# Rounding the last block's later weights in three products, with remainders on GpSimd, a tenth extra expert tile and filling matmuls in the router

## The reference, cut to what matters

```python
aff = softmax(h @ w_router)                      # 256 x 16
g, idx = top_k(aff.swapaxes(1, 2), 32)           # each expert takes 32 tokens
xs = h[idx]
y = (silu(xs @ w_gate[e]) * (xs @ w_up[e])) @ w_down[e] * g
x = x + g_f * scatter_add(y, idx)
```

```python
h = rmsnorm(x); x = x + concat(y_m, y_a) @ w_out           # y_m: mLSTM "hm", y_a: causal attention "oa"
h = rmsnorm(x)
q = rmsnorm(h @ wq_x);  k, v = (rmsnorm(mem) @ wkv_x)      # memory of 256 rows, k normed
x = x + softmax(q k^T) v @ wo_x
h = rmsnorm(x); x = x + square(relu(h @ w_ff1)) @ w_ff2    # width 4096
```

## Time and profile before

| | us |
|---|---|
| median of 3 runs | 1678.0 (1674.99 to 1681.05) |
| the profiled execution: its time | 1678.73 |
| its span, first to last instruction | 1676.9 |
| PE busy in the span | 1334.8 (80%) |
| DVE, ACT, POOL busy | 547.2, 348.4, 27.9 |
| bytes moved | 548.36 MB, mean 327 GB/s |
| mean granted clock of PE | 0.886 of full |

### The profile page before, as it was taken

How to read it: one execution, slowest core, us unless ns; L and a number is a source line. 1 busy time by engine, 2 the same in 40 slices (tenths; PEclk the granted TensorE clock), 3 DMA queues, 4 the chain that set the end, 5 groups by cost and what they waited for, 6 DMA issues and landing times.

```text
span 1676.9 us, 29699 instructions
## 1 busy us (share of the span) xinstructions
PE 1334.8 (80%) x12432; PEld 902.8 (54%) x12432; DVE 547.2 (33%) x1175; ACT 348.4 (21%) x616; POOL 27.9 (2%) x54
## 2 busy tenths in 40 slices
PE   4899996776676675789877667667667999899999
PEld 3798583432233232389734323223234888779997
DVE  2575664111000010147531101001013674455554
ACT  2412531000000000053400000000003332344443
POOL 2020100000000000000000000000000000000000
PEclk8999997988878778799989887787778999999999
DMA  9988798999999999994799999999999541355540
GB/s 341 356 278 305 257 404 359 418 422 422 422 422 422 422 422 422 413 360 163 268 381 417 422 422 422 422 422 422 421 421 390 197 133 33 126 176 181 195 152 26
DMA packets 145646, 548.36 MB, mean 327 GB/s; under 512 B 9711, under 2 KB 77713, under 8 KB 96297
## 3 DMA queue, kind: packets, MB, share of 16 engines
q1 hardware_dynamic: 142928, 542.97, 82.5%
q10 hardware_dynamic: 1080, 3.64, 0.6%
q0 software_dynamic: 1568, 0.77, 0.4%
HBM read 546.29 MB, written 1.05 MB: 326 GB/s over the span
## 4 chain that ended last, share of the span: by engine, by line
PE 44%; DMA 43%; DVE 7%; ACT 2%; issue 2%; SPq 1%; DVEq 0%; ACTq 0%
DMA ring<-in_moe_w_up 33%; PE bank L700 8%; DMA ring<-in_moe_w_down 7%; PE bank L526 6%; PE bank L804 6%; PE bank L566 5%; PE bank L1227 5%; PE bank L827 2%; PE bank L595 2%; DMA ring<-in_ada_w 1%; DMA ring<-in_w_in 1%; DMA ring<-in_attn_w_in 1%; DVE ring_split L1548 1%; PE bank L715 1%; PE bank L1156 1%
## 5 line engine op out<-in xcount | busy, mean ns | idle before, releaser
L804 PE MATMUL bank<-ring,scratch 128*32 128x256 f32 x3840 | 302.5, 467 | 144.3 <-DMA ring<-in_moe_w_up 100.8
L804 PEld LDWEIGHTS bank<-ring,scratch 128*32 128x32 f32 x3840 | 134.4, 129 | 296.8 <-DMA ring<-in_moe_w_up 153.9
L827 PE MATMUL bank<-ring,scratch 128*32 128x256 f32 x2016 | 159.9, 469 | 49.6 <-DMA ring<-in_moe_w_down 35.5
L1504 DVE COPY scratch<-bank 128x256 f32<-128x256 f32 x32 | 13.6, 424 | 432.9 <-PE bank L813 432.9
L700 PE MATMUL bank<-scratch_split,ring_split 128*128 128x256 f32 x1248 | 151.4, 283 | 3.7 <-DVE ring_split L1548 3.7
L700 PEld LDWEIGHTS bank<-scratch_split,ring_split 128*128 128x128 f32 x1248 | 150.5, 191 | 5.3 <-DVE ring_split L1548 4.1
L827 PEld LDWEIGHTS bank<-ring,scratch 128*32 128x32 f32 x2016 | 68.2, 132 | 135.0 <-DMA ring<-in_moe_w_down 63.3
L1548 DVE TENSOR_TENSOR ring_split<-ring,ring_split 128x2048 fp32r<-128x2048 f32 x48 | 110.1, 2293 | 75.8 <-ACT ring_split L2125 75.7
L2112 ACT ACTIVATE scratch<-bank 128x256 f32<-128x256 f32 x32 | 12.3, 383 | 485.0 <-PE bank L804 485.0
L526 PE MATMUL bank<-ring,hT 128*128 128x256 f32 (+1 forms) x512 | 111.7, 377 | 1.3 <-DVE hT L1315 0.7
L2125 ACT CAST ring_split<-ring 128x2048 fp32r<-128x2048 f32 x48 | 91.4, 1906 | 57.2 <-PE bank L1227 36.7
(11 more groups left out here) (443 smaller groups left out, 1441.1 us busy)
## 6 DMA issues: line engine op xcount, KB each, us to landing
ring<-in_moe_w_down SPq DMA_DIRECT2D x126, 1024.0 KB, 26.5
ring<-in_moe_w_gate SPq DMA_DIRECT2D x120, 1024.0 KB, 24.9
ring<-in_moe_w_up SPq DMA_DIRECT2D x120, 1024.0 KB, 26.7
ring<-in_ada_w SPq DMA_DIRECT2D x48, 1024.0 KB, 9.0
ring<-in_w_ff SPq DMA_DIRECT2D x32, 1024.0 KB, 5.3
ring<-in_conv_w_in SPq DMA_DIRECT2D x12, 1024.0 KB, 12.5
ring<-in_attn_w_in SPq DMA_DIRECT2D x10, 1024.0 KB, 11.2
ring<-in_w_in SPq DMA_DIRECT2D x7, 1024.0 KB, 11.8
```

Of the source, the lines that this page charges most:

```text
L804: mm = nc.tensor.matmul(GU[32 * j:32 * j + 32, m * 256:(m + 1) * 256], xs[:, k % 2, 16 * k - k % 2 * 16:16 * k - k % 2 * 16 + 32], W[:, (k ...
L827: mm = nc.tensor.matmul(Y[32 * g:32 * g + 32, 0:256], actT[:, b, 32 * j:32 * j + 32], W[:, b * D + g * 256:b * D + (g + 1) * 256], start=( ...
```

## The change

1. *The tenth tile.* `EXTRA` is 10. The tenth goes in two halves of 512 KB to where `take_w` was and to `gate`; `take_w` goes (the weights of one expert are multiplied straight from `take_p` and `aff`), and the experts' gate is kept in a tile of its own, `moe_gate`.
2. *The router.* Before each of PE's three waits in the router it runs filling matmuls of ident by 512 columns of x into bank 3, which nothing reads: 2, 5 and 1.
3. *The last block.* 18 pieces (`LATE`) of kvx, out2, qx and ox are multiplied the split way by `pe_late`. ACT rounds each piece (`round_late`), once its unit has landed and once the pieces have been read whose place the rounded numbers take (`LATE_BEHIND`: numbers of pieces); POOL subtracts (L2613); PE waits for POOL (`late_split`). The left factors are split as well: `rounded` on ACT and `rest_of_turned` on DVE stand where `turned` stood, ox's on ACT L2540. The norm of kx moves from behind attention b to its step 4, out2m.0 from step 6 to step 7, and out2m.1 behind the attention.

```diff
+LATE = [(("kvx", _u), 0, 8) for _u in range(4)] + [(("out2", _u), 0, 4) for _u in range(4)] + \
+       [(("out2", _u), 4, 4) for _u in range(4)] + [(("qx", _u), 0, 8) for _u in range(2)] + \
+       [(("ox", _u), 0, 4) for _u in range(4)]
+LATE_BEHIND = [(), (), (0,), (1,), (2,), (3,), (2,), (3,), (4,), (5,), (6,), (7,), (8, 10), (9, 11), (13,), (13,), (14,), (15,)]
...
+        def pe_late(pe, n, name, h, rows=None, ts=range(TT), bank=None):
+            key, k0, kk = LATE[n]
+            if 0 in ts:
+                sig("late_split").take(pe)
...
+            for i, (ht, wt) in enumerate(((h[0], hi), (h[0], lo), (h[1], hi))):
+                for k2 in range(0, kk, 2):
+                    if rows and i != 1:
+                        sig(rows[i // 2]).take(pe)
+                    for t in ts:
+                        for k in (k2, k2 + 1):
+                            mm = nc.tensor.matmul(T[:, t * 256:t * 256 + 256], ht[:, k, t * P:(t + 1) * P], wt[:, k, :],
...
@@ pe_moe @@
             done(f"lgn{l}", mm)
+            pe.wait_ge(free[3], turns[3])
+            def keep_clock(n):
+                for _ in range(n):
+                    nc.tensor.matmul(banks[3][:, :], ident, x[:, 0, 0:512], start=True, stop=True)
+            keep_clock(2)
             sig("aff_ready").take(pe)
...
+            keep_clock(5)
             sig("order_ready").take(pe)
...
+            keep_clock(1)
             sig("take_ready").take(pe)
...
@@ the product beside attention b, PE @@
-                    W = slot(pe, ("kvx", u), KD, 256)
...
+                    pe_late(pe, u, f"kvx.{u}", (mem_hi, mem_lo), ts=(t,))
-                elif i in (6, 8):
...
+                elif i == 7:
...
+                    pe_late(pe, 4, "out2m.0", (hm_hi, hm_lo))
...
@@ the experts' weights of a row, DVE @@
-                        for t in range(TT):
-                            ins = V.tensor_tensor(take_w[:, t, :, :], take_p[:, t, :, :],
...
-                        ins = V.tensor_copy(w_rep[:, :, j, :], take_w[:, :, e, :])
+                        ins = V.tensor_tensor(w_rep[:, :, j, :], take_p[:, :, e, :],
+                                              bc(aff[:, :, e].unsqueeze(2), [P, TT, CAP]), ALU.mult)
...
@@ last block, DVE @@
+            def rest_of_turned(name, given, lo, hi, mod, tiles, last=None):
...
+                        ins = V.scalar_tensor_tensor(out=lo[:, k, :], in0=T[:, k % 2 * SEQ:(k % 2 + 1) * SEQ],
+                                                     scalar=mod(k)[0], in1=hi[:, k, :], op0=ALU.mult, op1=ALU.subtract)
...
+            def beside_b(i):
+                if i == 1:
+                    rest_of_turned("hmT", "hm_hi", hm_lo, hm_hi, plain("m_out_g_2"), range(2))
+                elif i == 4:
...
+                    give("kx_ready", norm4(kx, sq2))
...
@@ last block, ACT @@
+            def rounded(name, given, hi, mod, tiles):
...
+                        ins = A.activation(hi[:, k, :], T[:, k % 2 * SEQ:(k % 2 + 1) * SEQ], ACT.Copy, scale=mod(k)[0])
...
+            def round_late(n):
+                key = LATE[n][0]
+                for m in LATE_BEHIND[n]:
+                    s.wait_ge(*late_read[m])
+                q, filled, _ = seating(seat[key])
+                s.wait_ge(landed[q], 16 * filled)
+                sig("late_hi").give(A.copy(late_hi(n), late_unit(n, ring)))
...
+                        if i == 4:
+                            roots(ss, 8)
+                            load_table(ACT.Exp)
+                        if i in (1, 4, 5, 6, 7):
+                            round_late(3 if i == 1 else i)
+                        if i == 7:
+                            part_out("out2m", 0, part2)
+                            round_late(8)
+                    if name == "c" and i in (2, 4):
+                        round_late(13 + i // 2)
...
+            rounded("n3", "h3_hi", h3_hi, plain("norm_x_g_2"), (2, 3))
+            round_late(12)
+            round_late(13)
...
@@ GpSimd @@
+            for n, (key, _, _) in enumerate(LATE):
+                q, filled, _ = seating(seat[key])
+                g.wait_ge(landed[q], 16 * filled)
+                sig("late_hi").take(g)
+                sig("late_split").give(nc.gpsimd.tensor_tensor(late_unit(n, ring_split), late_unit(n, ring), late_hi(n),
+                                                               ALU.subtract))
@@ SyncE: where the extra tiles go, and behind what @@
+        two_halves = (carve(S, 20, D), carve(GT, 0, D))
-            if isinstance(e, int) and e == 1 and s < EXTRA:
-                return extra[l][s], extra_landed[s], 16 * (l + 1)
+            if isinstance(e, int) and e == 1 and s < EXTRA - 1:
+                return whole(extra[l][s]), extra_landed[s], 16 * (l + 1)
+            if isinstance(e, int) and e == 1 and s == EXTRA - 1:
+                return two_halves, extra_landed[s], 32 * (l + 1)
-                    turn_of = ({4: (2, 3, 4), 8: (5,), SLOTS: (6, 7, 8)}, {TAIL: (3, 4), SLOTS: (5, 6, 7, 8)})[l]
+                    turn_of = ({4: (2, 3, 4), 8: (5,), SLOTS: (6, 7, 8, 9)}, {TAIL: (3, 4), SLOTS: (5, 6, 7, 8, 9)})[l]
-EXTRA = 9
+EXTRA = 10
```

More of the change, by code:

```diff
@@ L2363, in _ @@
             load_table(ACT.Exp)
+            round_late(2)
             keys_values(1)
[L2365 removed]
+            rounded("hmT", "hm_hi", hm_hi, plain("m_out_g_2"), range(2))
             def attend(name):
```

164 lines of the change are left out of this document (108 added, 56 removed).

## The result

The changed kernel takes 1703.4 us (median of 4 runs, 1702.0 to 1705.7) against 1678.7 us: a ratio of 1.0149 with a 95% interval of 1.0131 to 1.0166, 22 to 28 us slower. The forecast of 1691 us had the direction and half the size; its range ended at 1702.

A forecast was written before the change was run, and what follows sets the result against it. The prediction took the kernel as bound half by PE and half by DMA. It summed -5.6 + 3.1 + 8.2 + 0.3 + 6.8 = +12.8 onto 1678.7, less 0.7 for the median: 1691 us, range 1678 to 1702.

The forecast's parts named there:

- The tenth tile and the router: Heads of the two expert stages: the extra tile and filling matmuls win 5.6 us (0 to 7.3).
- it fills most of each gap: Expert stage heads: one more megabyte, 2.5 us at 420 GB/s, queued before expert 0 reads, covers most of the stream's standstill.
- (a): Last block, kvx.0 and kvx.1: kvx.0 done 1.25 us sooner without gain, kvx.1 wins 1.25 us.
- Nothing: kvx.0: its 1.25 us win no time, since PE then waits for qk_ready, which DVE gives at 1369.7.
- POOL and DVE block each other: Rival, qk stretch: DVE instructions with two SBUF operands wait for POOL's, 4.4 us late, 1695 us; chance 0.20.
- (b): Attention b: PE waits 2.2 us for kvx.2, also for kvx.3, yet ends the stretch near 1400.5, before at 1400.4.
- (c): Attention b with kx's norm inside: PE idle about 3.9 us, clock loss 2.0; together with kvx work +3.1 us (-1 to +5).
- as before: Attention b: despite waits for kvx.2 and kvx.3, PE ends this stretch near 1400.5 us against 1400.4.
- (d): qx: PE starts qx.0 9.4 us behind x_ready instead of 0.7, behind ACT's queue and POOL; +8.2 us (+3.9 to +10).
- (e): Attention c: casts at i = 2 and 4 fit into ACT gaps of 1.0 and 0.8 us; +0.3 us.
- (f): ox: casts and DVE's remainders delay the residual, PE idle 8.5 us, low clock 2.0; +6.8 us (+4.8 to +8).

The follow-up runs named there:

- the other pair: The three-pass products of the last block without tenth tile and filling matmuls, against the kernel before: 1707.2 us; beside it the changed kernel with both parts, 1703.4 us.
- the filled hole: Changed kernel with out2m.0 at step 5 of attention b and out2m.1 at step 7, their roundings one step earlier: 1703.8 us, 1.0125 of the kernel before.
- the remainders shortened: Changed kernel with GpSimd's remainders of kvx.2, kvx.3 and all out2 pieces made for 64 columns only: 1700.3 us, 1.0149 of the kernel before.
- the order alone: Changed kernel with ACT rounding ff1.0 ahead of ox.2 and ox.3, DVE taking ff1.1's remainder between residual parts: 1696.1 us, 1.0094 of the kernel before.
- the earlier cast: Changed kernel with ACT rounding qx.0 right behind the second part of turned x (n3.1) instead of behind all four: 1697.1 us, 1.0105 of the kernel before.

## Why the prediction was wrong

*The tenth tile and the router: too large.* Forecast -5.6, measured about -2.5 alone (-0.2 to -5.0), and 1707.2 - 1703.4 = 3.8 by the other pair. The step "it fills most of each gap" was right for the gap, wrong for the stage. Expert 1's tiles outside the ring free no slot when they are read. By SP's waits, ten tiles of expert 2 instead of nine can follow expert 0's reads, but the next tile waits in both kernels until expert 1's eleventh has been read. So the stream stands still before that instead, in 312 to 328 us. The tile only moves 2.5 us of standing still; what is won is what PE reads sooner.

*(a), kvx.0: "Nothing" is the step that failed.* GpSimd's instruction kept DVE out, and PE waited 8.4 us. Taking it away brought 8.7 us in the profile and 7 in the median. That was the rival "POOL and DVE block each other", which had 0.20 and 1695 us; with its 4.4 replaced by 8.7 the forecast would have been 1700. The rival had the mechanism and missed the size: it put GpSimd's work beside the squares from 1352 us on, but the casts came sooner, and both remainders met instructions of DVE that follow on each other. The length of the DVE instruction is no measure; each waits for what is left of GpSimd's. The Trainium skill ("SBUF — State Buffer", section "Who interferes with whom") says that a DVE instruction with two SBUF inputs contends with a GpSimd instruction that reads SBUF, and that the first to issue holds the shared ports for its whole length. The trace agrees: 4.00 and 4.43 us for 0.17.

A small error went the other way. Without the collisions x to qk takes 85.1 us, 1.2 less than before: ACT loads the Sqrt table for this norm 18 us ahead (at 1346.56), so that DVE waits 0.36 us for the root instead of 1.70, and the 1.25 us of kvx.0 that the sum had lost are won.

*(b) and (c), attention b: the waits right, the shares wrong.* Forecast +3.1. Without the first two collisions the stretches from qk to n3.3 lie 6.3 us over before's (8.6 + 51.0 + 16.5 against 69.8). The waits for kvx.2 and kvx.3 came (2.19 and 2.14 us in that profile; in the changed kernel PE was too late to meet the first), and so did the hole behind the two table loads (3.7 us for 3.9). But the filled hole showed that it is not what counts: DVE's norm of oa ends the stretch, and it stood 1.6 us behind a remainder (L1384, 2.30 us). With the remainders shortened the stretch lost 4.5 of its 5.6 us, which leaves about 1 for ACT's queue, net of what the shorter products win back. The forecast had it the other way round: nothing net for GpSimd's waits ("as before") and 3.1 for ACT's queue.

*(d), qx: right.* Forecast +8.2, measured +7.8; PE began 8.8 us behind its last turn instead of 0.5, the wait is ACT's queue and then GpSimd, the clock was low.

*(e): right*, +0.5 for +0.3. *(f), ox: right in kind*, +8.1 for +6.8; PE was idle 9.0 us (8.5), 0.4 of it because DVE's two remainders of feed-forward met GpSimd's last (5.03 us for 4.62), and the order alone brought back 9 us of the stretch.

Sum for the last block: forecast 18.4, measured 30.3. Of the 11.9 missing, 8.7 are the two collisions of (a), from which its 1.2 us go off, 3.2 are (b) and (c), 1.3 (f); (d) and (e) take 0.1 off. Open: why the median of the earlier cast fell by more than its stretch, and how the head's gain spreads over executions; the start of the last block lay between 1276.0 and 1284.5 us in the nine profiles with the tenth tile and the filling, and between 1283.4 and 1286.4 in three with neither.

## What to carry to other kernels

Before giving GpSimd an elementwise piece, list what DVE does in the same microseconds: each instruction with two SBUF sources waits for the end of the GpSimd instruction that runs, however small it is itself. Put such pieces beside DVE work that reads PSUM (attention c here), and keep the piece's producer off the tail of another engine's queue. And a stall of a stream at the head of a stage is only moved when one more tile is loaded ahead into a place that frees no slot when it is read: look for where the ring is full next. It shrinks only if the consumer also starts to read sooner.
